# Compressed keys' high and low parts in one 128-column score product, their halves summed on the vector engine

## The reference

```
kc = compress(k_cm, pos_c[0], w1_c[0], w2_c[0])      # 63 compressed keys of 64 numbers
m_c = cmp_end[None, :] <= qpos[:, None]
p_c = masked_softmax(einsum('bqkgd,bnkd->bqkgn', q, kc) * scale, m_c)
o_c = einsum('bqkgn,bnkd->bqkgd', p_c, vc)
return gates[..., 0:1] * o_c + gates[..., 1:2] * o_s + gates[..., 2:3] * o_w
```

## Time and profile before

| what | us |
|---|---|
| median of 3 runs (1929.72 to 1932.1) | 1931.26 |
| the profiled execution's own time | 1930.78 |
| its span | 1929.0 |
| PE busy, share of the span | 1868.6, 97% |
| DVE busy | 1147.4, 59% |
| ACT busy | 916.8, 48% |
| POOL busy | 481.1, 25% |
| period of the attention stage, 963.52 to 1026.10 | 62.58 |

### The profile page before, as it was taken

The page is one execution under the profiler, slowest core; times in us unless marked ns, Lnnn a source line. Parts: engine busy times, 40 slices in busy tenths (PEclk is TensorE's granted clock), DMA queues, the critical chain, the costliest instruction groups (busy, mean ns, idle before and its releaser), DMA issues.

```text
span 1929.0 us, 31985 instructions
## 1 busy us (share of the span) xinstructions
PE 1868.6 (97%) x11762; PEld 1678.3 (87%) x11763; DVE 1147.4 (59%) x1601; ACT 916.8 (48%) x1536; POOL 481.1 (25%) x640
## 2 busy tenths in 40 slices
PE   8999999999999989999999999999988999999997
PEld 8999978899999978889888888998856888888884
DVE  5544454632112448888888888644468586644756
ACT  3243431211110348788888888511023476545745
POOL 0000000000000215555555554002211244322433
PEclk9999999999999969999999999999999999999998
DMA  5233242243213400000000000534253798877865
GB/s 175 77 117 110 83 166 55 66 126 101 93 49 88 136 18 1 1 2 1 1 2 1 1 2 1 164 88 166 88 197 143 279 396 289 302 276 238 316 221 187
DMA packets 113736, 232.61 MB, mean 121 GB/s; under 512 B 25034, under 2 KB 81906, under 8 KB 107442
## 3 DMA queue, kind: packets, MB, share of 16 engines
q1 hardware_dynamic: 106162, 205.81, 30.4%
q0 software_dynamic: 7456, 25.17, 5.3%
HBM read 190.33 MB, written 42.71 MB: 121 GB/s over the span
## 4 chain that ended last, share of the span: by engine, by line
PE 56%; DVE 4%; ACT 1%; issue 1%; POOL 1%; POOLq 0%; ACTq 0%; DVEq 0%
PE ps L2977 20%; PE ps L2057 6%; PE ps L2036 6%; PE ps L2648 5%; PE ps L254 4%; PE ps L2011 3%; PE ps L2013 3%; PE ps L2965 1%; PE ps L2003 1%; DVE small L2111 1%; PE ps L3026 1%; PE ps L2062 1%; PE ps L1990 1%; PE ps L1989 1%; PE ps L2634 1%
## 5 line engine op out<-in xcount | busy, mean ns | idle before, releaser
L2111 DVE TENSOR_REDUCE small<-ps 128x1 f32<-128x640 f32 (+7 forms) x256 | 180.0, 704 | 42.8 <-PE ps L2003 41.4
L2135 DVE TENSOR_TENSOR turned_low<-ps,turned_high 128x512 fp32r<-128x512 f32 (+2 forms) x304 | 175.8, 614 | 10.1 <-ACT turned_high L2211 7.5
L2279 POOL TENSOR_SCALAR region_w<-region_w,small,gates 128x640 f32<-128x640 f32 (+7 forms) x172 | 141.0, 829 | 155.4 <-DVE small L2115 155.2
L2211 ACT CAST turned_high<-ps 128x512 fp32r<-128x512 f32 (+2 forms) x304 | 155.3, 532 | 48.7 <-PE ps L2036 46.0
L2011 PE MATMUL ps<-key_stacks,query_stacks 128*128 128x256 f32 (+3 forms) x384 | 142.6, 371 | 11.3 <-ACT region L2200 4.0
L2057 PE MATMUL ps<-turned_high,value_stacks 128*128 128x256 f32 (+1 forms) x608 | 152.8, 287 | 0.1
L2057 PE MATMUL ps<-turned_low,value_stacks 128*128 128x256 f32 (+1 forms) x608 | 142.5, 279 | 0.0
L2977 PE MATMUL ps<-gate_parts,rows_parts 128*128 128x512 f32 x552 | 131.6, 394 | 1.4 <-issue 1.4
L2200 ACT ACTIVATE region_w<-ps,small 128x640 f32<-128x640 f32 (+7 forms) x172 | 122.1, 710 | 19.7 <-DVE small L2111 15.3
L2977 PE MATMUL ps<-down_parts,hidden_parts 128*128 128x512 f32 x552 | 131.2, 393 | 0.0
L2977 PE MATMUL ps<-up_parts,rows_parts 128*128 128x512 f32 x552 | 128.9, 389 | 0.0
(11 more groups left out here) (507 smaller groups left out, 5028.3 us busy)
## 6 DMA issues: line engine op xcount, KB each, us to landing
region_k<-in_w_gate SPq DMA_DIRECT2D x16, 2048.0 KB, 9.7
region_k<-in_w_up SPq DMA_DIRECT2D x16, 2048.0 KB, 10.5
region_w<-in_w_down SPq DMA_DIRECT2D x16, 2048.0 KB, 12.9
region_w<-in_w_in SPq DMA_DIRECT2D x16, 512.0 KB, 4.3
small<-gate_a SPq DMA_DIRECT2D x8, 516.0 KB, 3.4
region_w<-gate_b SPq DMA_DIRECT2D x8, 516.0 KB, 3.9
region_k<-in_x_prompt SPq DMA_DIRECT2D x8, 512.0 KB, 7.6
region_k<-in_w_in SPq DMA_DIRECT2D x8, 512.0 KB, 4.4
```

The source lines that it names most:

```text
L2111: nc.vector.tensor_reduce(nmax[:, n % 4:n % 4 + 1], sc, AX.X, ALU.max, negate=True).then_inc(s_max, 1)
L2135: nc.vector.tensor_tensor(lo, m.ps[:, turn_bank(G), 0:w], hi, ALU.subtract).then_inc(s_lo, 1)
L2211: nc.scalar.copy(hi, m.ps[:, turn_bank(G), 0:w]).then_inc(s_hi, 1)
L2279: nc.gpsimd.tensor_scalar(probs(H, t), probs(H, t), rec[:, H % 4, t:t + 1], m.gates[:, 2 * p + t, col:col + 1], ALU.mult, ALU.mult).then_i ...
```

## The change

The two compressed key tiles become one, `compressed_keys` (`kc`) of 2 x 64 columns for each group, high parts in columns 0 to 63 and low parts in 64 to 127. One product of 128 columns gives both partial scores side by side instead of two products of 64 that accumulate. A call's four tiles now need 4 x 2 x 128 = 1024 columns, two banks, and so the call is cut in halves s = 0 and 1 of two tiles each; half s goes into the spare bank of job (H, s), behind that job's scores. DVE adds the two partial scores of each half with a reduction (`compressed_sum`, 252 results from 504 inputs) out of PSUM into `pc_rows`; maximum, clamp and subtraction then read `pc_rows` in SBUF. `free_scores` waits for the sum of the half instead of the subtraction. In DVE's order the maximum and subtraction come behind the second half's sum, behind the second maximum of H+2; `compressed_gain` of H+1 comes behind the second maximum of H+2. In ACT's order the compressed Exp comes one iteration of H later. POOL clears one tile of 256 columns instead of two of 128.

```diff
-        self.kc1 = self.sb("compressed_key_stacks", [P, NKV, 64], F32R)
-        self.kc2 = self.sb("compressed_key_lows", [P, NKV, 64], F32R)
+        self.kc = self.sb("compressed_keys", [P, NKV, 2 * 64], F32R)
+        self.kc1, self.kc2 = self.kc[:, :, 0:64], self.kc[:, :, 64:128]
...
-    def compressed_bank(c):
-        return scores_bank(n_of[16 * (c // 2) + 4 * (c % 2), 0]) + 1
+    def compressed_bank(c, s):
+        return scores_bank(n_of[16 * (c // 2) + 4 * (c % 2), s]) + 1
...
-                if t == 0 and compressed_ahead(H):
-                    pe.wait_ge(s_cd, compressed_of(H) + 1)
+                if compressed_ahead(H):
+                    pe.wait_ge(s_ch, 2 * compressed_of(H) + t + 1)
...
-        def compressed_scores(c):
+        def compressed_scores(c, s):
...
-            for r in range(4):
-                i = 4 * (c % 2) + r
+            for r in range(2):
+                i = 4 * (c % 2) + 2 * s + r
...
                 for g in range(NKV):
-                    out = m.ps[:, bank, r * P + g * 64:r * P + g * 64 + 64]
-                    nc.tensor.matmul(out, qs[:, g, tile], kc1[:, g, :], start=False, stop=False, skip_group_check=True)
-                    last = nc.tensor.matmul(out, qs[:, g, tile], kc2[:, g, :], start=False, stop=(g == 1),
+                    out = m.ps[:, bank, r * 256 + g * P:r * 256 + (g + 1) * P]
+                    last = nc.tensor.matmul(out, qs[:, g, tile], kc[:, g, :], start=False, stop=(g == 1),
                                             skip_group_check=True)
...
             if H + 2 < NHALF and compressed_ahead(H + 2):
-                compressed_scores(compressed_of(H + 2))
+                compressed_scores(compressed_of(H + 2), 0)
             for G in todo[0:1]:
                 turn(G)
             if H + 2 < NHALF:
                 scores(H + 2, 1)
+            if H + 2 < NHALF and compressed_ahead(H + 2):
+                compressed_scores(compressed_of(H + 2), 1)
...
+        def compressed_sum(c, s):
+            q = c % 2
+            parts = m.ps[:, compressed_bank(c, s), :].rearrange("p (x h n) -> p x n h", h=2, n=64)
+            dve.wait_ge(s_cs, 2 * c + s + 1)
...
+            at = 8 * q + 4 * s
+            nc.vector.tensor_reduce(pc_rows[:, at:at + 4, 0:NCMP], parts[:, :, 0:NCMP], AX.X, ALU.add).then_inc(s_ch, 1)
...
-            nc.vector.tensor_tensor(pc_rows[:, 8 * q:8 * q + 8, 0:NCMP], sc,
-                                    cmax.unsqueeze(2).to_broadcast([P, 8, NCMP]), ALU.add).then_inc(s_cd, 1)
+            nc.vector.tensor_tensor(sc, sc, cmax.unsqueeze(2).to_broadcast([P, 8, NCMP]), ALU.add).then_inc(s_cd, 1)
...
             if H + 2 < NHALF and compressed_ahead(H + 2):
-                compressed_max(compressed_of(H + 2))
+                compressed_sum(compressed_of(H + 2), 0)
...
+            if H + 2 < NHALF:
+                job_max(H + 2, 1)
+            if H + 2 < NHALF and compressed_ahead(H + 2):
+                compressed_sum(compressed_of(H + 2), 1)
+                compressed_max(compressed_of(H + 2))
             if 0 <= H + 1 < NHALF and compressed_ahead(H + 1):
                 compressed_gain(compressed_of(H + 1))
-            if H + 2 < NHALF:
-                job_max(H + 2, 1)
...
             for G in todo[1:2]:
                 high(G)
-            if H + 2 < NHALF and compressed_ahead(H + 2):
-                compressed_probs(compressed_of(H + 2))
+            if 0 <= H + 1 < NHALF and compressed_ahead(H + 1):
+                compressed_probs(compressed_of(H + 1))
```

More of the change, by code:

```diff
@@ L1529, in _ @@
             nc.gpsimd.memset(q_flat, 0.0).then_inc(s_zero, 1)
-            for t in (m.kc1[:].rearrange("p g n -> p (g n)"), m.kc2[:].rearrange("p g n -> p (g n)"), m.vc_stacks.rearrange("p g d -> p (g d)")):
+            for t in (m.kc[:].rearrange("p g n -> p (g n)"), m.vc_stacks.rearrange("p g d -> p (g d)")):
                 nc.gpsimd.memset(t.bitcast(F32), 0.0).then_inc(s_kz, 1)
@@ L1713, in _ @@
                 keep(A)
-            act.wait_ge(s_kz, 3)
+            act.wait_ge(s_kz, 2)
             act.wait_ge(s_end, 1)
@@ L1811, in _ @@
                 keep(A)
-            dve.wait_ge(s_kz, 3)
+            dve.wait_ge(s_kz, 2)
             dve.wait_ge(s_kch, 1)
@@ L1942, in attend_prompt @@
     s_cmax, s_csum, s_cgain = m.sem("a_c_max"), m.sem("a_c_sum"), m.sem("a_c_gain")
-    s_cs, s_cd, s_cp = (m.sem("a_c_" + n) for n in ("scores", "differences", "probs"))
+    s_cs, s_ch, s_cd, s_cp = (m.sem("a_c_" + n) for n in ("scores", "sums_of_parts", "differences", "probs"))
     s_t, s_hi, s_lo = lw.s_turned, m.sem("a_turned_high"), lw.s_low
```

21 lines of the change are left out of this document (11 added, 10 removed).

## The result

The changed kernel takes 1937.49 us (median of 7 runs, 1935.13 to 1938.01), the kernel before, run beside it, 1931.03 (7 runs, 1929.72 to 1932.1). The ratio is 1.0036, with a 95% interval of 1.0027 to 1.0045: 6.5 us slower, where 1938 us was forecast. The profiled execution took 1937.72 us, 6.9 more than the profiled one before; its span is 1935.9.

What follows compares the result with a forecast made beforehand. PE leads (97% busy), but DVE's lows, which PE waits for, set the cost. 7 x 1.3 + 0.4 - 8 x 0.3 = +7.1 us on 1930.78 gives 1937.9, median 1938 us; range 1930 to 1946.

Steps and rivals of the forecast that it cites:

- place 2: Half-head 16j-1: DVE waits for the Exp moved later on ACT, delaying the lows; +1.3 us per period net with Place 1.
- What PE saves: Compressed score products: a call falls from 1.95 to 1.08 us, saving PE 0.87 per call, 13.9 us in 16 calls.
- the rival that the change doesn't do what it says: 128 columns cost PE twice 64, nothing saved; about 0.3 us a period, 1940, inside the forecast, no own chance.
- What DVE pays: Two PSUM sums per call at 0.683 us, maximum at 0.658: DVE gains 1.34 us per call, 21.5 in 16 calls.
- the rival of the slow strided sum: DVE's sums take 1.03 us each because PSUM inputs lie 64 apart; 11 us more, 1949; chance 0.08.
- Place 1: Half-head 16j-2, even call: PE arrives 0.87 us earlier but waits 0.87 longer for the first low; net -0.1 us.
- Place 3: Half-heads 16j+2 and 16j+3, odd call: PE's wait for POOL goes, a wait for the low comes; net -0.3 us.
- A period at full clock: One of the eight repeats of the prompt attention: 62.58 us before, 63.6 us forecast.
- The clock: Rival: longer PE waits near 967 and 972 lower the clock once each period; 5.5 us more, 1943.4; chance 0.10.
- The first period: PE at half clock, POOL's order sets the pace, gain about 0.4 us later: +0.4 us in place of +1.3.
- The faster rival: PE keeps its saving if ACT reaches Exp before DVE wants it; 1927.7, or 1921 with half kept; chance 0.12.

Runs made afterwards that it cites:

- the first experiment: Changed kernel with the compressed Exp alone moved forward on ACT, to the end of the iteration in which the subtraction is made: 1921.64 us.
- the short sums: Changed kernel with DVE's sums over 8 of the 63 keys of each group, so other scores are stale: 1926.13 us.
- the version with the maximum behind two lows: Changed kernel with Exp behind the next iteration's first high, gain block behind the lows, and maximum, clamp and subtraction behind the first two lows: 1919.14 us.

## Why the prediction was right

The forecast held, and the step that carried it was the right one: place 2, the Exp that DVE waits for. What was off were sizes and the clock, which cancelled; that the sum came out so close is luck.

- **What PE saves:** the block of compressed products fell from 1.95 us to twice 0.58, where 0.54 was said. The product of 128 columns occupies PE for 0.13 us instead of the 0.115 taken from another place of the trace, and the saving is 12.6 us in 16 calls, not 13.9. A product of 64 took 0.11, so the rival that the change doesn't do what it says falls.
- **What DVE pays:** 0.682 us for a sum, 0.678 for the maximum, 0.68 for the subtraction. The sum was priced right to 1 ns, and the rival of the slow strided sum falls. The Trainium skill, "Advanced Engine Details and Errata", PSUM Cachelines, gives PSUM lines of two fp32 values and says that non-contiguous access slows matmuls significantly. A reduction on DVE is not slowed here: 504 elements in pairs 64 apart take 0.682 us, where 504 neighbours took 0.683. The page says it of matmuls, and no run here shows a strided access of PE.
- **Place 1** (said -0.1, measured 0.0): PE's saving is given back as a wait of 1.27 us, some 1.3 were said. The clamp took 0.36 us instead of 0.17 (last section), which is more than the difference.
- **Place 2** (said +1.4 without place 1, measured +1.29): DVE idled 1.24 us for the Exp, 1.3 were said, and moving that one Exp took the cost out. It is a turn of PE that waits 1.23 us, not the values.
- **Place 3** (said -0.3, measured -0.5): PE's wait for POOL went and the one for the low came, as said. DVE's wait for the Exp at the odd call is 0.66, 0.8 was said.
- **A period at full clock:** +0.7 where the prediction had +1.0. This is the term that was mis-sized, by 0.1 us at place 2 and 0.2 at place 3 (and 0.1 at place 1 the other way). At full clock the six periods lose 6 x 0.73 = 4.4 us where 6.0 were said, and the last stretch, with a place 3 alone, 0.0 where it was to win 0.3.
- **The clock** was a rival with a chance of 0.10 and is partly true: in the six periods four falls of about 0.6 us, 2.3 in all, against 0.9 in the kernel before, and a fifth in the first period. With it the stage ends 7.3 us later, and the whole program 6.9, where 7.1 was summed. The rival was wrong on the place: I put the falls at 967 and 972, at the longer waits of places 1 and 2, and they come at place 3, which I had counted as a gain.
- **The first period** with one place 2 behind it: 0.4 + 1.3 - 0.3 = 1.4 said, +2.3 measured from the stage's first scores. The fall of the clock at 733.5 us is in it, some 0.6 if it cost what the others did (an estimate from the periods above). I had no clock in this term, and no run shows the 0.4 for the gain by itself.
- **The faster rival** was said to turn on whether ACT reaches the Exp before DVE wants it. That is what the first experiment did, and it gave 1921.64 us; the rival's figure with half of PE's saving kept was 1921. In the changed kernel as it stands it is false.

## What to carry to other kernels

Split a change into the work that it adds and removes and the order that it moves, and price them apart: here the change was 8 to 12 us faster than the kernel before once reordered, and one Exp queued six instructions later hid that. How much of it a better order alone would give the kernel before is not shown, as only one such order was tried. On an engine with a fixed queue, what a block needs has to be made so early that the queue never stops for it: that was worth 1.87 us a period here. Then the block may go behind the instructions that others wait for: 0.35 us a period at most, and nothing for a block that already lay in idle time. Idle time of an engine over a period (9.7 us here) says nothing on whether it is idle in front of what the bound engine needs.

## What the runs showed that was not expected

DVE and POOL came to wait for each other, by a new order in time and by an operand of DVE moved from PSUM to SBUF. The clamp of 8 numbers, whose operands are the old ones, by line in the changed kernel:

```profile
L2112 DVE TENSOR_SCALAR small<-small x8: 171/365/376, 714.1 to 1159.3; 128x8 f32<-128x8 f32 x8
```

It took 0.17 us in all eight calls before. Seven of the eight are long now, those that start while POOL casts queries (1031.09 to 1031.83 at the place shown); the first call has no cast beside it and took 0.17. With the short sums the same clamp starts just ahead of the cast instead, and in the version with the maximum behind two lows there is none beside it; it takes 0.17 us in all eight calls of both. The line with the short sums:

```profile
L2112 DVE TENSOR_SCALAR small<-small x8: 171/172/173, 712.1 to 1146.3; 128x8 f32<-128x8 f32 x8
```

And POOL's subtraction of the query lows, 0.72 to 0.75 us in the kernel before and mostly so here, took 1.24 in the seven cases in which it started 0.03 us behind DVE's subtraction, which now has both inputs in SBUF. The Trainium skill, "SBUF — State Buffer", Who interferes with whom, says that only the port pair that DVE and GpSimd share causes contention, and that it is an exclusive lock; the trace agrees, as either engine loses time according to who comes first. On the path it is 0.19 us at seven of the eight even calls, up to 1.4 us in all. No run removed it alone.

The clock: a wait of 1.27 us and one of 1.23 within 6 us (1033.32, 1038.91) didn't lower it in any version that has them, and waits of 0.80 and 0.65 us with 0.7 us of work between them were followed by a fall in some periods and not in others.
